# Convolution variances as columns: root and reciprocal on a few columns, spread by a product with the identity

## What is computed

```python
def layer_norm(x, g, b):
    xf = x.astype(jnp.float32)
    mu = jnp.mean(xf, axis=-1, keepdims=True)
    xc = xf - mu
    y = xc * lax.rsqrt(jnp.mean(xc * xc, axis=-1, keepdims=True) + EPS)
    return (y * g.astype(jnp.float32) + b.astype(jnp.float32)).astype(x.dtype)

def conformer_conv(u, conv_w, conv_b, ln_g, ln_b):
    val, gate = jnp.split(u, 2, axis=-1)
    a = val * jax.nn.sigmoid(gate)
    y = lax.conv_general_dilated(a, conv_w, ...)
    y = layer_norm(y + conv_b, ln_g, ln_b)
    return jax.nn.silu(y)
...
    attn_out = blocked_gqa_attention(q, k, v)
    conv_out = conformer_conv(u, conv_w, conv_b, conv_ln_g, conv_ln_b)
    mix = jnp.concatenate([attn_out, conv_out], axis=-1) @ w_out
    x = x + gate1 * mix
```

## Time and profile before

| | before |
|---|---|
| median of 3 runs | 1550.4 us |
| the profiled execution | 1550.12 us |
| its span, first to last instruction | 1548.1 us |
| mean granted clock of PE | 0.971 |
| PE busy | 1449.1 us (94%) |
| weight loads (PEld) | 1078.7 us (70%) |
| DVE busy | 1118.1 us (72%) |
| ACT busy | 799.0 us (52%) |
| POOL busy | 192.7 us (12%) |

### The profile page before, as it was taken

The page is one execution under the profiler, slowest core; times in us unless marked ns, Lnnn a source line. Parts: engine busy times, 40 slices in busy tenths (PEclk is TensorE's granted clock), DMA queues, the critical chain, the costliest instruction groups (busy, mean ns, idle before and its releaser), DMA issues.

```text
span 1548.1 us, 27140 instructions
## 1 busy us (share of the span) xinstructions
PE 1449.1 (94%) x10061; PEld 1078.7 (70%) x10061; DVE 1118.1 (72%) x1586; ACT 799.0 (52%) x1312; POOL 192.7 (12%) x210
## 2 busy tenths in 40 slices
PE   4999999889999989988399999999999999999996
PEld 1777787537878867765277777777777777777774
DVE  1258988898868876357677877778777787877774
ACT  2222232147777773232456666566665666655662
POOL 0022012200000001121101101211011211111110
PEclk9999999989999999998599999999999999999998
DMA  9400001453000002233878888988889898889951
GB/s 339 161 1 28 28 1 55 158 223 111 2 2 1 2 28 82 96 126 124 314 247 283 293 283 282 305 289 295 276 290 303 283 303 273 290 287 301 304 181 17
DMA packets 113682, 281.31 MB, mean 182 GB/s; under 512 B 10581, under 2 KB 16825, under 8 KB 110552
## 3 DMA queue, kind: packets, MB, share of 16 engines
q1 hardware_dynamic: 105944, 259.54, 47.5%
q0 software_dynamic: 7680, 20.98, 6.0%
HBM read 259.51 MB, written 20.97 MB: 181 GB/s over the span
## 4 chain that ended last, share of the span: by engine, by line
PE 83%; DVE 6%; ACT 6%; DMA 2%; issue 1%; POOL 1%; SPq 0%; ACTq 0%; DVEq 0%; POOLq 0%
PE banks L1434 11%; PE banks L1409 11%; PE banks L1414 10%; PE banks L1410 10%; PE banks L1094 8%; PE banks L1303 7%; PE banks L1105 6%; PE banks L1254 4%; PE banks L1231 4%; PE banks L1241 4%; ACT xs_t L973 2%; DVE c_t L1634 2%; DMA ada<-in_ada_w 2%; PE banks L1441 1%; PE banks L1467 1%
## 5 line engine op out<-in xcount | busy, mean ns | idle before, releaser
L1939 DVE TENSOR_TENSOR low<-raw,high 128x1024 fp32r<-128x1024 f32 x384 | 447.9, 1219 | 1.0
L952 ACT ACTIVATE high<-raw 128x1024 fp32r<-128x1024 f32 x384 | 380.5, 1052 | 0.8
L1634 DVE SCALAR_TENSOR_TENSOR c_t<-a_t,taps,c_t 128x256 f32<-128x256 f32 (+2 forms) x360 | 215.2, 663 | 0.5
L1409 PE MATMUL banks<-high,x_hi 128*128 128x512 f32 x512 | 208.5, 407 | 0.0
L1410 PE MATMUL banks<-high,x_lo 128*128 128x512 f32 x512 | 200.1, 391 | 0.0
L1414 PE MATMUL banks<-low,x_hi 128*128 128x512 f32 x512 | 158.6, 391 | 1.1 <-DVE low L1939 1.1
L1094 PE MATMUL banks<-h_t,w_u 128*128 128x256 f32 x640 | 144.0, 383 | 1.2 <-DVE h_t L1584 1.2
L1094 PEld LDWEIGHTS banks<-h_t,w_u 128*128 128x128 f32 x640 | 121.3, 192 | 17.2 <-issue 1.4
L1409 PEld LDWEIGHTS banks<-high,x_hi 128*128 128x128 f32 x512 | 96.1, 188 | 32.9 <-issue 13.6
L1434 PE MATMUL banks<-raw,xs_t 128*32 128x256 f32 x2048 | 118.7, 384 | 0.0
L1736 DVE TENSOR_REDUCE negmax<-banks 128x1 f32<-128x1024 f32 (+1 forms) x80 | 85.0, 1063 | 43.0 <-PE banks L1231 42.8
(11 more groups left out here) (223 smaller groups left out, 2198.5 us busy)
## 6 DMA issues: line engine op xcount, KB each, us to landing
raw<-in_w_gate SPq DMA_DIRECT2D x128, 512.0 KB, 4.6
raw<-in_w_up SPq DMA_DIRECT2D x128, 512.0 KB, 5.9
raw<-in_w_down SPq DMA_DIRECT2D x64, 1024.0 KB, 5.1
ada<-in_ada_w SPq DMA_DIRECT2D x24, 1024.0 KB, 8.3
w_u<-in_w_in SPq DMA_DIRECT2D x4, 1024.0 KB, 19.3
x_in<-in_x_prompt SPq DMA_DIRECT2D x4, 1024.0 KB, 5.0
w_out_sb<-in_w_out SPq DMA_DIRECT2D x1, 4096.0 KB, 13.7
x_again<-in_x_prompt SPq DMA_DIRECT2D x4, 1024.0 KB, 5.7
```

The costliest lines, as they stand in the source:

```text
L952: act.activation(high[c % RING][:, :], raw[ph][:, k, :], ACT.Copy).then_inc(hi_ready, 1)
L1409: pe.matmul(bank(b + h), s_hi_k, w_high[:, half], start=(k == 0), stop=False)
L1634: dve.scalar_tensor_tensor(out=c_t[s][:, c, :], in0=a_t[:, c, bass.ds(k + o, n)], scalar=taps[:, c, bass.ds(k, 1)], in1=c_t[s][:, c, :], o ...
L1939: dve.tensor_tensor(low[ph][:, k, :], raw[ph][:, k, :], high[c % RING][:, :].bitcast(F32), ALU.subtract).then_inc(lo_ready, 1)
```

## The change

The sum of squares is formed the other way round. The squares of 128 tokens are now the weights of the product and one column of ones is what moves, so that the variances of 128 tokens stand on the 128 partitions in one PSUM column: 2, 3 and 5 columns for the three spans. Root and reciprocal work on these columns. A new function `spread_rs` brings the inverse back to the layout of `c_t`: for each 128 tokens the column of inverses, read as if it stood 128 times side by side, is the weight, and the identity moves through it, so that every partition gets the row of 128 inverses, in the span's PSUM bank. The multiply of `scale_span` reads that bank instead of SBUF and is cut at the bank's 512 columns.

`spread_rs(0)` stands on PE ahead of `variance(1)`, `spread_rs(1)` behind the four gate rows, `spread_rs(2)` between the halves of the projection of tile 0. DVE waits for a new semaphore, `rs_spread`, between reciprocal and multiply. `turn_x1` waits for the last multiply of span 2 instead of its root.

```diff
--- before.py
+++ after.py
@@ -319,6 +319,7 @@
         var_ready = sem("var_ready")
         root_ready = sem("root_ready")
         inv_ready = sem("inv_ready")
+        rs_spread = sem("rs_spread")
         scaled = sem("scaled")
         conv_out = sem("conv_out")
 
@@ -784,9 +785,9 @@
 
             def root(s):
                 act.wait_ge(var_ready, s + 1)
-                for b, c0, c1 in STAT_BANK[s]:
-                    last = act.activation(rt_c[s][:, c0:c1], bank(b)[:, 0:c1 - c0], ACT.Sqrt, scale=1.0 / DC, bias=eps_col[:, :])
-                last.then_inc(root_ready, 1)
+                nt = SPANS[s][1] // P
+                act.activation(rt_c[s][:, 0:nt], bank(STAT_BANK[s][0][0])[:, 0:nt], ACT.Sqrt, scale=1.0 / DC,
+                               bias=eps_col[:, :]).then_inc(root_ready, 1)
 
             def silu_span(s):
                 for c in range(CC):
@@ -1168,10 +1169,21 @@
 
             def variance(s):
                 pe.wait_ge(squared, CC * (s + 1))
-                for c in range(CC):
-                    for b, c0, c1 in STAT_BANK[s]:
-                        last = pe.matmul(bank(b)[:, 0:c1 - c0], ones[:, :], sq_c[s][:, c, c0:c1], start=(c == 0), stop=(c == CC - 1))
+                pe.wait_ge(centred, CC * (s + 1))
+                for i in range(SPANS[s][1] // P):
+                    for c in range(CC):
+                        last = pe.matmul(bank(STAT_BANK[s][0][0])[:, i:i + 1], sq_c[s][:, c, P * i:P * (i + 1)], ones[:, 0:1],
+                                         start=(c == 0), stop=(c == CC - 1))
                 last.then_inc(var_ready, 1)
+
+            def spread_rs(s):
+                pe.wait_ge(inv_ready, s + 1)
+                for b, c0, c1 in STAT_BANK[s]:
+                    for o in range(c0, c1, P):
+                        i = o // P
+                        last = pe.matmul(bank(b)[:, o - c0:o - c0 + P], rs_c[s][:, i:i + 1].to_broadcast([P, P]), ident[:, :],
+                                         start=True, stop=True)
+                last.then_inc(rs_spread, 1)
 
             def mod_row(out, row, bias_row, c, n):
 
@@ -1200,6 +1212,7 @@
             variance(0)
             for k in range(4, 6):
                 mod_step(1, k, ada2[k], 2)
+            spread_rs(0)
             variance(1)
             for k in range(6, KC):
                 mod_step(1, k, ada2[k], 2)
@@ -1207,6 +1220,7 @@
             pe.wait_ge(bias_rows_loaded, 32)
             for n in range(4):
                 gate_row(n)
+            spread_rs(1)
             for k in range(KC):
                 mod_step(2, k, ada2[k], 3)
             pe.wait_ge(mod_ready, 2)
@@ -1341,9 +1355,11 @@
             pe.wait_ge(pick_made, 3)
             for p in range(NPAIR - 1):
                 project_out(2 * p, 0)
+                if p == 0:
+                    spread_rs(2)
                 project_out(2 * p, 1)
                 if p:
-                    pe.wait_ge(root_ready, 3)
+                    pe.wait_ge(scaled, 3 * CC)
                     turn_x1(p - 1)
                 if p >= 2:
                     turn_logits(p - 2)
@@ -1704,11 +1720,14 @@
 
             def scale_span(s):
                 dve.wait_ge(root_ready, s + 1)
-                dve.reciprocal(rs_c[s][:, :], rt_c[s][:, :]).then_inc(inv_ready, 1)
-                dve.wait_ge(inv_ready, s + 1)
+                nt = SPANS[s][1] // P
+                dve.reciprocal(rs_c[s][:, 0:nt], rt_c[s][:, 0:nt]).then_inc(inv_ready, 1)
+                dve.wait_ge(rs_spread, s + 1)
                 dve.wait_ge(squared, CC * (s + 1))
                 for c in range(CC):
-                    dve.tensor_tensor(c_t[s][:, c, :], c_t[s][:, c, :], rs_c[s][:, :], ALU.mult).then_inc(scaled, 1)
+                    for b, c0, c1 in STAT_BANK[s]:
+                        last = dve.tensor_tensor(c_t[s][:, c, c0:c1], bank(b)[:, 0:c1 - c0], c_t[s][:, c, c0:c1], ALU.mult)
+                    last.then_inc(scaled, 1)
 
 
             dve.wait_ge(u_gated, CC * NPAIR)
```

## The result

The changed kernel took 1567.47 us (median of 6 runs, 1558.58 to 1568.6) against 1549.96 for the kernel before (6 runs, 1548.73 to 1552.12): a ratio of 1.0097 with a 95% interval of 1.0078 to 1.0116. Run again beside the experiments it took 1562.66 us (6 runs, 1556.65 to 1567.74) against 1550.43, ratio 1.0080 [1.0063, 1.0097]. Both medians are slower than before and above the forecast of 1559 and its upper end of 1561.5.

The account below looks back on a forecast made before the run. TensorE was taken to hold 83% of the chain, with VectorE leading stretch A and TensorE stretch B. 1550.1 + 4.0 + 4.7 = 1558.8, with the 0.3 about 1559; own range 1556 to 1561.5, wider range from 1551.0.

Parts of the forecast that it names:

- The price of a one-column product: Variance and spread products on PE: each instruction costs 0.11 us at full clock and 0.21 at half.
- Rival 3: Weight loads cost only 0.06 us each: net -0.7, about 1549.5 us; chance 0.06.
- The reciprocals: DVE's reciprocals fall to about 0.2 us each: 3.8 us leave A but become a wait for PE; B gains nothing.
- A: Stretch of about 320 to 352 us, spans 0 and 1, up to attention's first maximum; +0.3 at steady full clock.
- The choice on which the forecast hung: In both variance stretches on PE, one-column products neither hold nor raise the clock; this gives +4.0 in A, +4.7 in B.
- Rival 1: The clock holds because weight loads count as work: +0.3 in A and +1.1 in B, 1551.5 us; chance 0.22.
- B: Stretch of 577 to 617 us, span 2: variance 2 and the output projection, bound by PE.
- Rival 2: The clock holds in only one of the two stretches: +4.3 to +5.1, about 1555 us; chance 0.13.
- Term B: Variance 2 and projection at half clock: variance 1.5, projection 2.1, spread 1.1, sum +4.7 us, range 4.0 to 5.5.
- Term A: Clock falls in variance 1, delaying ada steps and gate rows: first maximum 4.0 us late, range 2 to 5.4.
- the 5.4 of the slip inside the gate rows: In A, if the copy's pause breaks the return, the clock comes back 3.6 into the gate rows, losing 1.8 more.
- The range's upper end: Whole kernel: 1561.5 us, the top of the forecast's own range, with A at 2 to 5.4 and B at 4.0 to 5.5.

Follow-up runs that it names:

- the best version: Change for spans 0 and 1 only, with 96-column variance products and gate-row bias products on 128 rows, span 2 as before: 1546.4 us against 1550.55, ratio 0.9974.
- The experiment with short reciprocals: Kernel before with reciprocals cut to 2, 3 and 5 columns, multiply reading the root, no spread: 1549.35 us, ratio 0.9990.
- with 96 columns in B: Kernel before with the change for span 2 only, its variance products moving 96 columns instead of one: 1551.2 us, ratio 1.0012.
- B alone: Kernel before with the change for span 2 only, spans 0 and 1 as before: 1558.67 us, ratio 1.0044.
- the changed kernel with full rows: Changed kernel with the gate rows' bias products on 128 rows instead of 8, the other 120 zero: 1556.08 us, ratio 1.0037.
- A alone: Kernel before with the change for spans 0 and 1 only, span 2 as before: 1559.06 us, ratio 1.0045.

## Why the prediction was right in its cause and wrong in its size

- **The price of a one-column product: right.** 0.11 at full and 0.21 us at half clock were taken; 40 took 8.69 us at half clock, 0.217 each, and the 16 of variance 0 took 1.95 at full, 0.12 each. Rival 3, loads at 0.06, is out.
- **The reciprocals: right for A, with a gain behind it left out.** 0.17 us, and what they freed turned into a wait for PE: 9.01 us ahead of the multiply of span 1 in the changed kernel, and still 2.09 in the best version, where the clock holds. The experiment with short reciprocals puts their worth at 0.9 us of A. What the prediction didn't see is behind A: where DVE's maximum comes close behind PE's first scores, PE waits less ahead of its second ones, and the traces are 2.4 to 2.7 us shorter up to variance 2.
- **The choice on which the forecast hung: right.** The clock falls during variance 1 and does not rise during variance 2, with PE busy 2.00 of 2.00 us. The Trainium skill, "TensorE: Matmul & The Clock Gate", "Part 1: The HAM clock gate", sets the clock by how busy PE has been recently; the 0.55 of 332 to 334 and the 0.50 of 588 to 590 show that being occupied was not enough here. Rival 1, the clock that holds, did not come about by itself, but its price for B was right: with 96 columns in B the loss was 1.1 us, as it said. Its 0.3 for A no run shows by itself. Rival 2, a fall in one stretch only, is seen in no trace of the changed kernel: both of them lose in A and in B. (By the prediction's own terms its price was 5.0 to 5.1, 0.3 + 4.7 or 4.0 + 1.1, and not from 4.3 on.)
- **Term B: right.** 4.7 was predicted; 5.5, 4.7, 4.8 and 5.5 us were measured in the two traces of the changed kernel, in B alone and in the changed kernel with full rows. Its parts in the changed kernel: variance 1.8 (predicted 1.5), projection 2.6 (8.06 against 5.45, a sixth of the earlier trace rows's 32.69; predicted 2.1), spread 1.1.
- **Term A: wrong in size, and this is the step that failed.** "If the clock is back 3.6 to 4.8 us after 331.9, the gate rows run their 8.35 at full clock", from which 4.0 was taken, with 5.4 as the end. I treated the gate rows as dense work that runs at full clock from its start and holds it. In neither trace of the changed kernel did they. In the second the clock came back only at 340, 2.7 us into the gate rows and 7.9 us after variance 1, then held, and A was 5.2 us longer: the 5.4 of the slip inside the gate rows, and not the 4.0. In the first it came back at 339, ahead of them, and was lost again at 346 within them, which made A 6.8 us longer. In A alone it came back behind them, at 357, and A was 13.2 longer. With all 128 rows A was 3.7 longer, which looks like the 4.0, but 1.4 us of that is the quicker rows; at the old length it would be 5.1 (an estimate), about what the second trace lost. The total of that version, 1556.1, lies at the forecast's own lower end with the help of these 1.4 and of the 2.7 behind A. The timeline of before calls the bias products 8*128, so that they differ from the wide products could have been seen; that the clock is lost in them more easily for it is likely, but not shown apart from their length.
- **The range's upper end** had only the course that the profile of before happened to show. The gate rows could lose the clock in unchanged code too, as the trace of B alone shows, so before's A was a favourable case and not a fixed sum. The changed kernel's slower runs (1567 to 1569) were not profiled; that they are falls of A alone's kind is an inference from their clock, 0.958 to 0.960, and from their size: with A alone's 49.1 instead of 42.7 the first trace's 1562.4 would be 1568.8 (an estimate). The two profiled runs, 1562.4 and 1556.65, don't show the miss of the medians by themselves: the first lost 3.3 us ahead of anything changed, which is chance, and both won back 2.6 to 2.7 at the first scores, which no term of the forecast has. What carries the medians beyond the range are the slower runs, and their course is in no trace.

## What to carry to other kernels

Swapping the sides of a product so that one column moves does not shorten it when the other side becomes one wide weight load per block, and the matrix engine then does so little per load that its clock can fall in the work that follows. Before pricing work behind such a stretch at full clock, look at the traces of several executions: the gate rows here brought the clock back in some, lost it in others, and a single profile showed only one course. And price a shorter operation by what waits right behind it: 3.8 us off VectorE were worth 0.9 in that stretch, since TensorE stood that close.

## What the runs showed of the hardware that was not expected

- Gate rows in which half of the instructions read 8 of 128 rows didn't treat TensorE's clock the same way each time: half clock through all four in A alone, a fall from 1.00 to 0.50 inside them in four traces of nine, two of these in unchanged code, and a return inside the first row that then held in the changed kernel's second trace. With 128 rows, 120 of them zero, the clock was lost in none of four traces.
- Such an f32 row was also slower at full clock: four instructions of 256 columns took 1.05 us with 8 rows and 0.86 with 128.
- With TensorE idle for 2.56 and 3.91 us ahead of its second scores the clock stood at 0.50 behind the wait; with 1.64 us, in eleven traces, it stayed at 1.00.
- With TensorE equally busy, 1 and 32 moving columns left variance 2 at half clock to its end, 8.7 us; with 96 the clock came back in it, and it took 6.7 to 7.7. So padding idle columns with work that nobody reads took 11.5 us off.
